# Two transformer-like blocks on one core: turned rows loaded two units later, the end split over two engines

## The reference, cut to what matters

```python
x = x + 0.5 * rmsnorm(swiglu(rmsnorm(x, g[0]), w_in, w_out), g[1])     # feed-forward
x = x + rmsnorm(mixer(rmsnorm(x, g[2])), g[3])                          # attention, or a state-space model
x = x + 0.5 * rmsnorm(swiglu(rmsnorm(x, g[4]), w_in, w_out), g[5])     # feed-forward
gate = sigmoid(rmsnorm(x, g[6]) @ w_gate)
x = x + rmsnorm(gate * (p @ w_proj), g[7])

def swiglu(h, w_in, w_out):
    gu = h @ w_in
    return (silu(gu[..., :2816]) * gu[..., 2816:]) @ w_out
```

## Time and profile before

| | |
|---|---|
| median of 3 runs | 1628.22 us (1627.43 to 1628.95) |
| the profiled execution | 1630.51 us, its span 1628.4 us |
| PE busy | 1596.6 us, 98% of the span |
| DVE busy | 1141.1 us, 70% |
| ACT busy | 928.1 us, 57% |
| POOL busy | 173.4 us, 11% |
| granted PE clock | 0.998 of full speed |
| DMA | 329.54 MB, mean 202 GB/s |
| turned rows, write | 60 of 256 KB, median 3.7 us to landing |
| turned rows, loads | 240 of 64 KB, median 2.3 us to landing |
| weights | 528 of 512 KB, median 4.7 us to landing |

### The profile page before, as it was taken

The page is one execution under the profiler, slowest core; times in us unless marked ns, Lnnn a source line. Parts: engine busy times, 40 slices in busy tenths (PEclk is TensorE's granted clock), DMA queues, the critical chain, the costliest instruction groups (busy, mean ns, idle before and its releaser), DMA issues.

```text
span 1628.4 us, 22833 instructions
## 1 busy us (share of the span) xinstructions
PE 1596.6 (98%) x8719; PEld 1340.0 (82%) x8719; DVE 1141.1 (70%) x1627; ACT 928.1 (57%) x1559; POOL 173.4 (11%) x240
## 2 busy tenths in 40 slices
PE   9999999999999999999999999999999999999997
PEld 7878899887878788888878887788889989788886
DVE  5566667788886766979776666756667776676655
ACT  6455556655567686553465555645555544655545
POOL 0000001126600102910010001000000000000000
PEclk9999999999999999999999999999999999999999
DMA  7787554576766576662567765677755434576762
GB/s 255 264 272 242 181 168 138 163 241 228 226 215 201 205 239 199 202 200 104 189 214 242 234 217 195 191 247 252 231 170 186 152 108 133 180 249 227 225 215 93
DMA packets 131949, 329.54 MB, mean 202 GB/s; under 512 B 15144, under 2 KB 52480, under 8 KB 131840
## 3 DMA queue, kind: packets, MB, share of 16 engines
q1 hardware_dynamic: 131392, 327.45, 61.6%
q0 software_dynamic: 160, 0.52, 0.1%
q10 hardware_dynamic: 288, 0.11, 0.0%
HBM read 310.16 MB, written 17.86 MB: 201 GB/s over the span
## 4 chain that ended last, share of the span: by engine, by line
PE 79%; DVE 10%; ACT 5%; DMA 3%; issue 2%; POOL 0%; SPq 0%; POOLq 0%; DVEq 0%; ACTq 0%
PE PS L2247 76%; DVE wlo L1413 2%; DVE wlo L1407 2%; DMA raw<-in_w 1%; DVE SC L1767 1%; PE PS L2392 1%; ACT whi L809 1%; ACT SC L1033 1%; DMA blocks<-wk 1%; PE PS L2250 1%; ACT whi L813 1%; DVE wk L1597 0%; ACT wk L849 0%; PE PS L2688 0%; DMA wk<-blocks 0%
## 5 line engine op out<-in xcount | busy, mean ns | idle before, releaser
L1413 DVE SCALAR_TENSOR_TENSOR wlo<-raw,ct,whi 128x512 fp32r<-128x512 f32 (+1 forms) x552 | 419.0, 807 | 192.1 <-ACT whi L813 191.6
L2247 PE MATMUL PS<-whi,xhi 128*128 128x512 f32 (+1 forms) x1312 | 500.4, 391 | 9.5 <-DVE wlo L1413 3.4
L2247 PE MATMUL PS<-wlo,xhi 128*128 128x512 f32 (+1 forms) x1312 | 495.0, 387 | 0.0
L813 ACT ACTIVATE whi<-raw,ct 128x512 fp32r<-128x512 f32 (+1 forms) x552 | 376.1, 734 | 193.8 <-PE PS L2247 139.6
L1407 DVE TENSOR_TENSOR wlo<-raw,whi 128x1024 fp32r<-128x1024 f32 x240 | 299.8, 1255 | 188.9 <-ACT whi L809 187.9
L2247 PE MATMUL PS<-whi,xlo 128*128 128x512 f32 (+1 forms) x1312 | 405.1, 387 | 0.0
L809 ACT ACTIVATE whi<-raw 128x1024 fp32r<-128x1024 f32 x240 | 252.3, 1057 | 227.8 <-PE PS L2247 181.6
L2247 PEld LDWEIGHTS PS<-whi,xhi 128*128 128x128 f32 x1312 | 245.6, 188 | 67.9 <-DVE wlo L1413 5.7
L2247 PEld LDWEIGHTS PS<-whi,xlo 128*128 128x128 f32 x1312 | 246.4, 188 | 50.5
L2247 PEld LDWEIGHTS PS<-wlo,xhi 128*128 128x128 f32 x1312 | 246.4, 188 | 49.1
L2247 PE MATMUL PS<-whi,hhi 128*128 128x512 f32 x544 | 173.3, 392 | 0.0
(11 more groups left out here) (287 smaller groups left out, 1458.7 us busy)
## 6 DMA issues: line engine op xcount, KB each, us to landing
raw<-in_w SPq DMA_DIRECT2D x528, 512.0 KB, 4.7
blocks<-wk SPq DMA_DIRECT2D x60, 256.0 KB, 3.7
wk<-blocks SPq DMA_DIRECT2D x240, 64.0 KB, 2.3
gr<-in_rows SPq DMA_DIRECT2D x14, 512.0 KB, 3.9
SC<-scratch SPq DMA_DIRECT2D x5, 512.0 KB, 7.7
X<-in_x SPq DMA_DIRECT2D x2, 512.0 KB, 5.3
SC<-scratch SPq DMA_DIRECT2D x4, 256.0 KB, 5.2
xn<-in_sc SPq DMA_DIRECT2D x2, 512.0 KB, 5.8
```

The lines of the kernel that those rows point to most:

```text
L813: e = a.activation(hi[:, f], src[:, f], ACT.Copy, scale=ct[:, c:c + 1])
L1413: e = v.scalar_tensor_tensor(lo[:, f], src[:, f], ct[:, c:c + 1], hi[:, f].bitcast(f32), MUL, SUB)
L2247: return pe.matmul(o, l, r, start=start, stop=stop)
```

## The change

The loads of turned rows stand two units later in SyncE's order, behind `up_at(n, j) + 13`. On ACT and DVE the turned rows of pair j - 1 are split behind i = 3 for every j above 1. At the beginning PE runs 7 and 6 products of zeros for 12 and 12, and ACT and DVE put the split of unit 1 between the two evictions of the second half of x. In gate 1 the second half of tokens runs its products with `xhi` first as well. At the end ACT takes sums of squares between the gates, DVE adds to X right behind each product, the last quarter's norm is made in two steps (times g on DVE, times the root on ACT), and the last 128 rows are stored in one transfer.

```diff
-        MOVES[up_at(n, j) + 11] = (moved(n, j), True)
+        MOVES[up_at(n, j) + 13] = (moved(n, j), True)
...
@@ sync
-            for h in range(2):
-                for i, f in enumerate((LO, HI)):
-                    q.wait_ge(s_xn, n_two(STORED, h, i))
-                    sp.dma_start(out[0, 128 * h:128 * h + 128, f], xn[:, h, f]).then_inc(s_out, 16)
-            sp.wait_ge(s_out, 64)
+            for i, f in enumerate((LO, HI)):
+                q.wait_ge(s_xn, n_two(STORED, 0, i))
+                sp.dma_start(out[0, 0:128, f], xn[:, 0, f]).then_inc(s_out, 16)
+            q.wait_ge(s_xn, n_two(STORED, 1))
+            sp.dma_start(out[0, 128:256, :], xn[:, 1, :]).then_inc(s_out, 16)
+            sp.wait_ge(s_out, 48)
...
@@ scalar, start(0)
-                    evict_hi(k, 1)
+                    evict_hi(k, 1, (0,))
                     use(v0 - 2)
+                    evict_hi(k, 1, (1,))
...
@@ scalar and vector, ffn
-                        if j > 1 and i == (3 if j == 2 else 2):
+                        if j > 1 and i == 3:
                             hidden_hi(j - 1)
...
@@ scalar, the end
-            for h in range(2):
-                sigmoid(STORED, h)
-            for h in range(2):
-                squares2(STORED, h)
+            sigmoid(STORED, 0)
+            sigmoid(STORED, 1, (0,))
+            squares2(STORED, 0, (0,))
+            sigmoid(STORED, 1, (1,))
+            squares2(STORED, 0, (1,))
+            squares2(STORED, 1)
+            q.wait_ge(s_yg, n_yg(STORED - 1, 1) + 1)
+            q.wait_ge(s_r2, n_one(STORED, 1))
+            q.wait_ge(s_xn, n_two(STORED, 0))
+            a.activation(xn[:, 1, HI], xn[:, 1, HI], ACT.Copy, scale=r2[STORED][1]).then_inc(s_xn, 1)
...
@@ vector, start(0)
-                    evict_lo(k, 1)
+                    evict_lo(k, 1, (0,))
                     use(v0 - 2)
+                    evict_lo(k, 1, (1,))
...
@@ vector, the end
                     gated(STORED, h, i)
-                add_x(STORED, h)
-            for h in range(2):
-                norm(STORED, h)
+                    add_x(STORED, h, (i,))
+            q.wait_ge(s_X, n_x(STORED, 1))
+            v.tensor_tensor(xn[:, 1, HI], X[:, 1, HI], row_in(ROW_G2[STORED])[:, HI], MUL).then_inc(s_yg, 1)
+            norm(STORED, 0)
+            norm(STORED, 1, (LO,))
...
@@ tensor, run(..., late=False)
-                        if h:
+                        if h and not late:
                             q.wait_ge(s_xlo, n_ev(by_half, h, 0))
-                    for low in (False, True) if by_half is not None and not h else (None,):
+                    for low in (False, True) if by_half is not None and (late or not h) else (None,):
...
-                    linear("gate1", x_acts, 4, head=2, tail=2, by_half=k, between=lambda: transposed(k, 1))
+                    linear("gate1", x_acts, 4, head=2, tail=2, by_half=k, between=lambda: transposed(k, 1), late=True)
...
@@ tensor, the program
-            nil_products(12)
+            nil_products(7)
             start(0)
-            nil_products(12)
+            nil_products(6)
```

More of the change, by code:

```diff
@@ L849, in squares, with sigmoid @@
                     a.activation(wk[:, f], y[:, f], ACT.Square, scale=sc, accum_out=ss[:, i:i + 1]).then_inc(s_sq, 1)
-            def sigmoid(k, h):
+            def sigmoid(k, h, cols=(0, 1)):
                 s = gate_of(k, h)
-                for i, f in enumerate((LO, HI)):
+                for i in cols:
+                    f = (LO, HI)[i]
                     if k == 6:
@@ L865, in load_table, with squares2 @@
                 a.activation(warm, mh[:, 0:1], f)
-            def squares2(k, h):
+            def squares2(k, h, cols=(0, 1)):
                 ss = ss2[k][h]
@@ L1486, in times_g, with add_x @@
                 v.tensor_tensor(y[:, HI], y[:, HI], g1[:, HI], MUL).then_inc(s_yg, 1)
-            def add_x(k, h):
+            def add_x(k, h, cols=(0, 1)):
                 if k == 0:
@@ L1506, in add_x, with norm @@
                     v.scalar_tensor_tensor(X[:, h, f], src[:, f], by, X[:, h, f], MUL, ADD).then_inc(s_X, 1)
-            def norm(k, h):
+            def norm(k, h, cols=(LO, HI)):
                 g2 = row_in(ROW_G2[k])
@@ L1512, in norm @@
                     q.wait_ge(s_tr, n_tr(k - 1, h))
-                for f in (LO, HI):
+                for f in cols:
                     v.scalar_tensor_tensor(xn[:, h, f], X[:, h, f], r2[k][h], g2[:, f], MUL, MUL).then_inc(s_xn, 1)
@@ L2257, in weight, with run @@
                 return whi[:, u % NSPLIT, :], wlo[:, u % NSPLIT, :]
-            def run(parts, base, last, by_half=None, finish=None, step=2, between=None):
+            def run(parts, base, last, by_half=None, finish=None, step=2, between=None, late=False):
                 for h in range(2):
@@ L2297, in run, with linear @@
                                 e.then_inc(s_used, 1)
-            def linear(name, acts, base=0, head=1, tail=1, by_half=None, finish=None, ready=None, n_fill=1, step=2, between=None, after=None):
+            def linear(name, acts, base=0, head=1, tail=1, by_half=None, finish=None, ready=None, n_fill=1, step=2, between=None, after=None, late=False):
                 kts = len(acts)
@@ L2310, in linear @@
                     first = by_half is not None and ks[0] == 0
-                    run(parts, base, ks[-1] == kts - 1, by_half if first else None, finish if first else None, step, None if ks[0] else between)
+                    run(parts, base, ks[-1] == kts - 1, by_half if first else None, finish if first else None, step, None if ks[0] else between, late)
                     if first:
```

## The result

The changed kernel takes 1677.7 us (median of 4 runs, 1673.0 to 1681.4) against 1628.6: ratio 1.029, 95% interval 1.0262 to 1.0318. I had said slower, by 4.9 us; it is 49 us. The profiled execution took 1673.04 (span 1670.9), 42.5 us more span than the profiled one of before, and that is what the traces have to explain.

The account below looks back on a forecast made before the run. PE, busy for 98% of the span, was taken to bound the kernel. Moved loads +5.7 us, beginning 0, gate 1 0 and end -0.8 gave +4.9, so the median 1628.22 becomes 1633.1 us; range 1624.4 to 1640.

Parts of the forecast that it names:

- the mechanism of unit 11: Block 1: pair 0's rows come later, split 11 behind them ends at 44.83, PE wanted it at 42.90: +1.9 us.
- The first has the same neighbour, so I take 5.1 for pair 0 ... and I take 5.4: Time taken by the four loads at their new place: 5.1 us for pair 0, 5.4 for pair 1.
- part 1: Loads of turned rows issued two units later: +5.7 us over the blocks, about +15 if loads take 6.1 us.
- Rival C: Loads of turned rows take more than 5.5 us each, since three units are ahead: +12, 1640 us; chance 0.15.
- PE wanted it at 53.78: Block 1, pair 1: split 15 ends at 57.25, PE wanted it at 53.78, so PE is 3.5 us behind.
- No PE wait for line 1597 in block 1: Block 1: PE's three waits for the gated product in the banks end, a gain of 2.2 us.
- Later pairs have three units between issue and use: 0: Pairs after the first two of a block have 8 us between issue and use, so they cost 0.
- Part 2, 0: Beginning, fewer products of zeros and xhi/split order exchanged: 0 us, bounds 0 and -0.8, or +1.5 if the clock rises later.
- Rival D: Beginning: PE's clock comes up later behind seven products of zeros, +1.5 us at most; chance alone 0.03.
- Part 3, 0: Gate 1: PE starts about 0.85 us earlier but waits for the second low part: 0, between 0 and -0.85.
- Part 4, -0.8: End: last normalisation 1.4 us earlier, 0.6 lost to one 512 KB transfer: -0.8 us, between -1.4 and 0.
- SyncE's wait under 40 us: SyncE's wait before line 561, for the write of the turned rows, falls from 119 us to under 40.

Follow-up runs that it names:

- s4: The changed kernel with the splits of unit 11 and 15 made ahead of the reads of pair 0's and pair 1's rows: 1673.4 us, ratio 1.0296.
- s3: The changed kernel with pairs 0 and 1 of every block loading behind unit 11 of a pair again, later pairs left moved: 1632.8 us, ratio 1.0046.
- s1: The changed kernel with the loads of turned rows behind unit 11 again and their readers at i = 2: 1628.6 us, ratio 0.999.
- s11: The changed kernel with the loads behind unit 11 again, readers kept at i = 3: 1632.3 us, ratio 1.0021.
- s6: The changed kernel with the four loads issued right ahead of unit 13 instead of right behind it: 1644.9 us, ratio 1.0085.
- s12: Kernel before with the new beginning and gate 1 order, loads from pair 2 on ahead of unit 13, readers as before: 1630.4 us, ratio 1.0007.
- s7: The changed kernel with eight products of 512 columns ahead of unit 11's in blocks 1 to 4: 1682.8 us, ratio 1.0324.
- s10: The changed kernel with pair 1 of every block loading behind unit 15 again, pair 0 and later pairs left moved: 1657.9 us, ratio 1.0166.
- s13: s12 with ACT making the split of unit 151 ahead of one piece of side work in block 2: 1628.1 us, ratio 1.0002.

## Why the prediction was wrong

The sign held, and so did the mechanism of unit 11 (rows late, split 11 queued behind them; from ACT's copy to the end of that split it is 4.37 us again, 4.38 in my sum); the size did not, and for pair 1 I named the wrong wait. Going by its steps:

- *"The first has the same neighbour, so I take 5.1 for pair 0 ... and I take 5.4"*: this is the step that failed. The loads of the twelve first pairs took 6.0, 8.0, 7.2, 5.9, 9.0, 6.5, 8.0, 8.3, 7.0, 7.2, 7.2 and 7.6 us, 7.4 on average for pair 0 and 7.3 for pair 1. My case had one unit close ahead and the next 5.9 us ahead. At the new place two or three units go out in the last 3.3 us, and in eleven of the twelve the loads stand 0.37 us behind the last. All sixty pairs of the changed kernel, sorted by the number of units in the 3.3 us ahead of their loads: one, 4.7 to 6.1 us (nine pairs, median 5.3); two, 4.8 to 9.0 (35 pairs, 6.5); three, 6.5 to 9.1 (16 pairs, 7.8). The ranges overlap, so the count is not all of it, but the median grows by more than 1 us with each unit. In the kernel before, with the last unit 6.5 us ahead, it was 3.2. I had written the burst down for pair 1 and priced it from a case without one. The measured sums of both pairs are 24.9 us above the 10.5 per block that I used, and with them my own sum for part 1 becomes 5.7 + 24.9 = 30.6. By blocks that is 4.8, 4.1, 5.5, 7.3, 3.7 and 5.2 us, and the lag's steps in the table are 5.1 (the -2.3 included), 5.9, 4.8, 9.4, 3.6 and 7.2. Rival C named the cause and stopped at 12.
- *The rest, 42.7 - 30.6 = some 12 us*, had no term: about 6 of clock, 3.0 - 1.4 = 1.6 of wait at unit 53 of block 2, 1.1 ahead of it, 1.5 late in block 3; some 2 I cannot place. The clock did not enter part 1 at all; it was a rival only for the beginning.
- *"PE wanted it at 53.78"*: the wrong wait. The bank of unit 14 is due first, at 51.06 - 2.0 = 49.1 for the rows, against 53.78 - 4.38 = 49.4 by split 15. Only 0.3 us apart, so the size hardly suffered; but s4 shows that a repair aimed at the split moves little (1673.4 us for 1677.7).
- *"No PE wait for line 1597 in block 1"*, 2.2 us gained: the three waits went (the lag falls by 2.3), but the same wait came back at unit 14 with 2.55 us, more than the three together.
- *"Later pairs have three units between issue and use: 0"*: nearly. With them moved and pairs 0 and 1 not (s3) PE ends 4.1 us behind s1. Most of that is the readers' place: with the readers alone at i = 3 (s11) PE ends 3.5 us behind s1.
- *Part 2, 0*: PE's wait of 1.50 us is 1.01 in the changed kernel, and PE takes unit 11 0.3 earlier in s1. Rival D added nothing: in the changed kernel's trace the clock does come up later, at 5.9 us against 4.0 in the kernel before (3.9 in s1), but PE then waits 1.04 us for ACT's split of unit 0 and takes it at 8.61, against 8.68 before.
- *Part 3, 0*: right. The wait at gate 1 moved to the second pair of units, lag -0.8 and +0.8, in every kernel that has part 3. The changed kernel, to lay beside the earlier trace rows:

```profile
1042.22 0.74 PE L2261 MATMUL PS<-whi,xhi 128*128 128x512 f32 x2 [0.70 <-DVE xlo L1542]
```

- *Part 4, -0.8*: from the last gate (1619.39 before, 1617.93 in s1) to the end of the span 9.0 and 8.5 us: -0.5 in s1, -0.2 in the changed kernel. From the last gate to the last issue it is 6.5 before and 5.5 in s1, but from there the single 512 KB transfer takes 3.0 us to the end where 256 KB took 2.4. In s1:

```profile
1622.61 0.75 DVE L1525 SCALAR_TENSOR_TENSOR xn<-X,st,gr 128x512 f32<-128x512 f32 x1 [0.44 <-POOL st L681]
1622.65 0.72 ACT L1401 ACTIVATE xn<-xn,st 128x512 f32<-128x512 f32 x1 [1.79 <-POOL st L681]
1623.40 0.33 SPq L665 DMA_DIRECT2D out<-xn  x1
```

- *SyncE's wait under 40 us*: it is 0.6, and this is the heart of the case. While SyncE stood 119 us for the write, nothing went out behind the last unit, and the four small loads of the first pairs took 3.2 to 6.2 us, 4.1 on average. With the wait gone they were issued later and close behind two or three units, and ACT's 36.9 us of waiting became 149. That it was the wait which spaced the queue I read from these rows; no run moves the loads and keeps a wait ahead of them, and s6 shows only that one unit less ahead of them is worth 1.7 us.

The rule of the Trainium skill that I had cited ("DMA: Bandwidth & Descriptors", "Queues, rings and completion order": each DMA engine takes descriptors in ring order) agrees with s6 and with the rows above.

## What to carry to other kernels

A wait on the issuing engine can be what keeps the queue short for the small transfer behind it; before it is removed, list what will then stand in the two or three microseconds ahead of that transfer, and price it from a row with as many units as close ahead, not from one with the same nearest neighbour. Work out for every consumer the moment at which its data stop being early, through banks and products too, and not at the first split alone: here the pair with 0.2 us to spare decided, while the eight later pairs of every block, moved with their readers, cost 4.1 us over the whole run (s3). Small transfers go ahead of the big one that is issued with them: that alone brought back 33 of the 49 us (s6).

## What the runs showed of the hardware that I had not expected

- The four 64 KB loads on a queue of their own took 7.3 and 9.7 us beside three units of 512 KB each on SyncE's queue, longer than in SyncE's own queue behind one or two (3.8 and 5.4 in s6).
- In the changed kernel PE's granted clock fell to 1.2 GHz for 3.4 us at seven waits of 2.4 to 3.8 us, from 0.4 us before to 1.4 us after PE's first product behind the wait. It did not at the waits of 3.36 us from 1103.1 and 2.55 us from 55.8. At unit 53 of block 2 it fell at 1.9 us in s12 and not in s6, and at 2.5 us in the changed kernel and not in s4, so the length of one wait does not settle it. What does stays open.
- In the profiled executions of s7, s10 and s12 PE runs 27 us at 1.2 GHz near 740 to 790 us, among small products (64 columns) where little is loaded, and is 11.1 us later behind it. The wait ahead of it, 0.9 us, is there without the fall too (735.43 in s12, 737.12 in the kernel before). Times that much above the others come in the kernel before as well (3 of 17 beside s13, at a mean clock of 0.99). I found no cause.
